# One product for the dilated values of both weight chunks, and the latent keys and values computed behind it

## What is computed

```python
dq, dk, dv, sq, sk, sv, iq, ik, iw, cq, ckv, kr = split_cols(x @ w_in)      # w_in: 1024 x 2920
...
rel = jax.nn.relu(jnp.einsum('bqhe,bse->bqhs', iqb, ik))                     # indexer, 8 heads
score = jnp.einsum('bqh,bqhs->bqs', iwb, rel)
_, idx = lax.top_k(score, n_sel)                                             # n_sel = 128
...
kv = (rms_norm(ckv, kv_norm) @ w_ukv).reshape(B, S, N_HEADS_MLA, MLA_NOPE + MLA_V)
k_nope, v = kv[..., :MLA_NOPE], kv[..., MLA_NOPE:]
```

## Time and profile before

| | us |
|---|---|
| median of 3 runs (lowest, highest) | 2184.23 (2182.27, 2187.38) |
| the profiled execution's own time | 2186.5 |
| its span in the trace | 2184.7 |
| TensorE busy | 2080.8 (95%) |
| VectorE busy | 1642.6 (75%) |
| ScalarE busy | 1409.2 (65%) |
| GpSimd busy | 581.3 (27%) |

### The profile page before, as it was taken

How to read it: one execution, slowest core, us unless ns; L and a number is a source line. 1 busy time by engine, 2 the same in 40 slices (tenths; PEclk the granted TensorE clock), 3 DMA queues, 4 the chain that set the end, 5 groups by cost and what they waited for, 6 DMA issues and landing times. The chain is left out here.

```text
span 2184.7 us, 32260 instructions
## 1 busy us (share of the span) xinstructions
PE 2080.8 (95%) x10998; PEld 1689.3 (77%) x10998; DVE 1642.6 (75%) x2419; ACT 1409.2 (65%) x1778; POOL 581.3 (27%) x336
## 2 busy tenths in 40 slices
PE   6999989899999999999888999898999999999996
PEld 4778878688888888887376888777888888888862
DVE  2486453699999999998345944537999999999955
ACT  3443762488888888887045347426888888888841
POOL 0010200133443444442011021002344434434310
PEclk9999999999999999999999999999999999999998
DMA  6312213599999999995741140265999999999938
GB/s 202 97 30 72 113 67 147 196 378 377 389 378 379 375 387 386 382 382 223 302 145 59 51 162 1 76 252 192 382 378 393 378 375 382 376 382 380 379 128 359
DMA packets 136052, 572.78 MB, mean 262 GB/s; under 512 B 32356, under 2 KB 58468, under 8 KB 82712
## 3 DMA queue, kind: packets, MB, share of 16 engines
q1 hardware_dynamic: 99096, 504.37, 60.5%
q0 software_dynamic: 36864, 67.19, 8.0%
HBM read 560.41 MB, written 78.14 MB: 292 GB/s over the span
## 5 line engine op out<-in xcount | busy, mean ns | idle before, releaser
L1430 POOL DMA_INDIRECT rows<-x_rows,index x122 | 281.4, 2307 | 129.8 <-issue 69.5
L1587 DVE TENSOR_TENSOR w_next_lo<-w_next,w_hi 128x2048 fp32r<-128x2048 f32 x128 | 292.8, 2288 | 0.1
L1587 DVE TENSOR_TENSOR w_lo<-w,w_hi 128x2048 fp32r<-128x2048 f32 x124 | 285.2, 2300 | 2.0 <-ACT w_hi L1635 1.4
L1635 ACT CAST w_hi<-w 128x2048 fp32r<-128x2048 f32 x124 | 236.4, 1906 | 51.0 <-PE ps_sum L1493 51.0
L1635 ACT CAST w_hi<-w_next 128x2048 fp32r<-128x2048 f32 x128 | 243.5, 1902 | 35.4 <-PE ps_sum L1493 35.4
L1491 PE MATMUL ps_sum<-w_hi,rowsT_first_hi 128*128 128x512 f32 x512 | 208.8, 408 | 9.1 <-PEq L151 9.1
L1491 PE MATMUL ps_sum<-w_hi,rowsT_hi 128*128 128x512 f32 x512 | 208.0, 406 | 4.4 <-DVE rowsT_lo L1599 4.4
L1516 PE MATMUL ps_sum<-w_hi,hiddenT_hi 128*128 128x512 f32 x512 | 201.8, 394 | 3.9 <-DVE hiddenT_lo L1606 3.9
L1493 PE MATMUL ps_sum<-w_hi,rowsT_first_lo 128*128 128x512 f32 x512 | 202.9, 396 | 0.0
L1493 PE MATMUL ps_sum<-w_hi,rowsT_lo 128*128 128x512 f32 x512 | 202.3, 395 | 0.0
L1518 PE MATMUL ps_sum<-w_hi,hiddenT_lo 128*128 128x512 f32 x512 | 201.8, 394 | 0.0
(11 more groups left out here) (286 smaller groups left out, 5283.3 us busy)
## 6 DMA issues: line engine op xcount, KB each, us to landing
w_next<-exp_w SPq DMA_DIRECT2D x192, 1024.0 KB, 10.1
w<-exp_w SPq DMA_DIRECT2D x128, 1024.0 KB, 9.6
w_first<-exp_w SPq DMA_DIRECT2D x32, 1024.0 KB
w_last<-exp_w SPq DMA_DIRECT2D x32, 1024.0 KB
wbuf<-w_in SPq DMA_DIRECT2D x16, 1024.0 KB, 5.5
got<-y_rows SPq DMA_DIRECT2D x8, 2048.0 KB, 21.3
got<-y_rows SPq DMA_DIRECT2D x16, 1024.0 KB, 24.3
w_out_sb<-w_out SPq DMA_DIRECT2D x2, 4096.0 KB, 19.3
```

The lines of the kernel that those rows point to most:

```text
L1430: pool.indirect_dma_start(rows[0:CAP, x.slot, :], None, d["x1_rows"], bass.IndirectOffsetOnAxis(ap=index[0:CAP, x.step, 0:1], axis=0), bou ...
L1587: dve.tensor_tensor(w13_lo[x.slot][:, :, k, :], w13[x.slot][:, :, k, :], w13_hi[:, :, k, :].bitcast(F32), ALU.subtract).then_inc(S["up_lo_ ...
L1635: act.copy(w13_hi[:, :, k, :], w13[x.slot][:, :, k, :]).then_inc(S["up_hi_b" if half else "up_hi_a"], 1)
```

## The change

Three things are edited. The `dv` units of both chunks become one: per block of 128 tokens, each product takes the 2 x 192 columns of chunks 8 and 9 together, out of both slots of `w_hi` or `w_lo`. The `kn` and `mv` units leave their places between the `idx` pairs and stand between `dv` and `sqk`. And `LOWER_AT` puts `lower(10)` and `lower(11)` at later rounds. Since both slots are now read until the last `dv` unit, `split_after` names that unit for chunk 10 and for chunk 11.

```diff
     latent = [("mq", t, c) for t in range(NT) for c in range(2)]
-    latent += [("kn", h) for h in range(H_MLA)] + [("mv", t) for t in range(NT)]
...
-    u += [("dv", c, t) for c in range(2) for t in range(NT)]
+    u += [("dv", t) for t in range(NT)]
+    u += [("kn", h) for h in range(H_MLA)] + [("mv", t) for t in range(NT)]
...
-LOWER_AT = {(3, 8): 7, (2, 0): 8, (2, 7): 9, (2, 15): 10, (1, 8): 11}
+LOWER_AT = {(3, 8): 7, (2, 0): 8, (2, 7): 9, (1, 11): 10, (1, 13): 11}
...
-    split_after = {last_use[c - 2]: c for c in range(2, len(CHUNKS))}
-    split_after[place[("rest", 0, 1)]] = 1
+    last_use[8] = last_use[9]
+    split_after = {u: [c for c in range(2, len(CHUNKS)) if last_use[c - 2] == u] for u in last_use.values()}
+    split_after[place[("rest", 0, 1)]] = [1]
...
+                    elif kind == "dv":
+                        n, rows = CHUNKS[c][1], slice(x[1] * P, (x[1] + 1) * P)
+                        both = out[:, 0:2 * n].rearrange("p (b c) -> p b c", b=2)
+                        for k in range(KD):
+                            v_hi, v_lo = w_hi[:, :, k, 0:n], w_lo[:, :, k, 0:n]
+                            pe.matmul(both, xT_hi[:, k, rows], v_hi, start=(k == 0), stop=False)
+                            pe.matmul(both, xT_hi[:, k, rows], v_lo, start=False, stop=False)
+                            mm = pe.matmul(both, xT_lo[:, k, rows], v_hi, start=False, stop=(k == KD - 1))
...
-                        o = act.copy(sb["dv"][:, x[2], x[1] * 192:x[1] * 192 + 192], src[:, 0:192])
+                        o = act.copy(sb["dv"][:, x[1], :], src[:, 0:2 * CHUNKS[8][1]])
...
-                    if u in split_after:
-                        upper(split_after[u])
+                    for c in split_after.get(u, []):
+                        upper(c)
```

More of the change, by code:

```diff
@@ L311, in _projections @@
     chunk_of = {"rest": lambda x: x[1], "ik": lambda x: IK_CHUNK, "iq": lambda x: 3 + x[1] // 2,
-                "dqk": lambda x: 5 + x[1] // 2, "dv": lambda x: 8 + x[1], "sqk": lambda x: 10 + x[1] // 2,
+                "dqk": lambda x: 5 + x[1] // 2, "dv": lambda x: 9, "sqk": lambda x: 10 + x[1] // 2,
                 "sv": lambda x: 12}
     last_use = {chunk_of[x[0]](x): u for u, x in enumerate(units) if x[0] in chunk_of}
-    split_after = {last_use[c - 2]: c for c in range(2, len(CHUNKS))}
-    split_after[place[("rest", 0, 1)]] = 1
+    last_use[8] = last_use[9]
+    split_after = {u: [c for c in range(2, len(CHUNKS)) if last_use[c - 2] == u] for u in last_use.values()}
+    split_after[place[("rest", 0, 1)]] = [1]
     with ExitStack() as ctx:
@@ L393, in _ @@
                             mm = pe.transpose(out[:, t * P:(t + 1) * P], x_sb[:, t, x[1]::KD], ident)
-                    elif kind in ("rest", "dv", "sv"):
+                    elif kind == "dv":
[6 more added lines that the diff above has]
+                            mm = pe.matmul(both, xT_lo[:, k, rows], v_hi, start=False, stop=(k == KD - 1))
+                    elif kind in ("rest", "sv"):
                         t = x[-1]
```

## The result

| | before | changed |
|---|---|---|
| median (lowest, highest), us | 2184.44 (2182.27, 2187.38) | 2220.63 (2219.93, 2220.67) |
| ratio, 95% interval | | 1.0164 [1.0146, 1.0182] |
| profiled execution, span | 2184.7 | 2218.6 |

What follows compares the result with a forecast made beforehand. TensorE was taken to bound the projections. Cheaper `dv` products, moved `kn` and `mv`, two new waits and low clock put `sqk` at 196.65 against 180.39, 16.3 us a layer: 2184.2 + 32.5 = 2217, range 2206 to 2226.

Steps and rivals of the forecast that it cites:

- TensorE sets the end, and its losses arrive: In the projections TensorE, busy 90.8 of 93 us, sets the end; everything it loses or gains arrives there.
- Products of `dv`: Joined `dv` products of 384 columns, 0.17 us apart, take 16.3 us: 5.2 us less work a layer.
- `kn` and `mv`: Taking them out of the `idx` stretch moves, not saves, 8.8 us of TensorE: 1.04 a `kn`, 0.64 an `mv`.
- First wait: Ahead of `dv`, TensorE stands from 152.0 to 161.4 until `lower(9)` has split chunk 9: 9.4 us.
- earlier selection: After the score sums, VectorE's selection starts at about 122.4 instead of 125.29: 2.9 us earlier.
- TensorE's arrival: TensorE reaches `dqk` at about 116.3 instead of 121.93, 5.6 us earlier, and ends `krT` at 152.0.
- Second wait: Ahead of `mv` 2, TensorE idles some 7 us while ScalarE's `upper(11)` waits for chunk 11, `kn` copies behind it.
- Clock: Behind each wait TensorE runs at the 1.2 GHz level, 1.5 us more; lasting twice as long would give 2220 to 2223.
- The sum: `sqk` begins at 196.65 against 180.39, 16.3 us a layer, 32.5 for two: 2184.2 + 32.5 = 2217.
- Two layers: Layer 1 is taken as a repeat of layer 0, so 16.3 us is doubled to 32.5.
- Only the first wait: Rival: chunk 11 lands while TensorE still has banks, `sqk` starts at 188.0, 7.6 late: 2199; chance 0.08.
- Sums blocked entirely: Rival: GpSimd holds VectorE's 384-wide sums off entirely; selection and `sqk` come 4.9 us later than forecast: 2227; chance 0.07.

Runs made afterwards that it cites:

- the version with only the keys: Changed kernel with only `kn` between `dv` and `sqk`, `mv` back between `idx` pairs, GpSimd's rotations after the last score sum, `lower(7)` to `lower(11)` earlier: 2173.80 us, ratio 0.9950.
- the run with both waits treated: Changed kernel with `lower(8)` to `lower(11)` at earlier rounds and `upper(11)` behind the last `mv` copy: 2189.02 us, ratio 1.0016.

## Why the prediction was right, point by point

- **TensorE sets the end, and its losses arrive.** Right. Layer 0's projections ended 18.74 us later, layer 1's 37.22; the forecast had 32.5 for both. The bounds worked out in the prediction, 12.8 to 25 us a layer, would be 2210 to 2234; the range it gives, 2206 to 2226, does not follow from them. The measured 2220.6 lies in both.
- **Products of `dv`.** Right. Predicted 0.17 us apart; four units copied 4.16 us apart, 24 x 0.173.
- **`kn` and `mv`.** Over-sized. Predicted 8.8 us, measured 7.7 (183.05 to 190.73 in the run with `upper(11)` later). The sum takes only two `mv` from it, 1.3 us, and those were right at full clock (1.2).
- **First wait.** The mechanism was right. It ended later than predicted, `dv` began at 163.43 instead of 161.4, and it was shorter, 7.9 us instead of 9.4, because TensorE itself came late (next point). What made its end late is the mis-sized term of the sum, the *earlier selection*: I had 2.9 us and measured 1.0 (124.28 against 125.29). Nearly half of the miss does not come from the change: the first 384-wide sum stood 0.85 later already, at 110.46 against 109.61. The rest is in the sums: I gave five of seven the slow rate and measured 7.75 us for seven, because rotations and sums kept each other busy longer. GpSimd is the cause, as the run with later rotations shows.
- **TensorE's arrival.** Predicted at `dqk` 116.3, measured 118.16, and the first products ran at clock 0.50. I had overlooked that pauses in the `idx` stretch could bring the low clock. It cost nothing at the end, because the first wait stood behind it; `krT` ended 3.5 us later than forecast, and the wait was the shorter for it.
- **Second wait.** Right, place and cause: VectorE reached `lower(10)` at 185.54 (183.5 predicted, late by the same term), 5.8 us later the chunk was there, and `mv` 2 began at 196.05 (193.85). The 1.9 us to spare between `upper(10)` and VectorE shrank to 0.4.
- **Clock.** I charged 1.5 us for the first wait. `dv` took 19.3 us behind it (163.43 to 182.74), against 16.8 in the version with only the keys (154.02 to 170.86), where no such stretch followed: 2.5 us. `dv` was so 1.5 us longer than the 17.8 forecast and used up 1.5 of the 1.9 us to spare. Anything beyond another 0.4 us would have arrived in the sum; that this under-sized term did not is in part luck. I charged 1.5 us for the second wait too. From 196.05 to 198.20 two `mv` took 2.15 us, 0.9 more than at full clock, and from there to the last copy it took 34.45 us, before 33.52: 0.9 more. Together 1.8.
- **The sum.** 196.65 predicted for `sqk`, 198.20 measured, 1.6 late; 0.9 of the clock came behind it. 16.3 + 1.6 + 0.9 = 18.8, the 18.74 of layer 0. Without the offset of 0.85 it is 17.9, and 36.4 for both layers, close to the 36.2 of the medians.
- **Two layers.** Layer 1 took 18.48 more. The span grew by 33.9, not 37.2: what follows the last `sv` copy of layer 1 took 893.91 us before and 890.59 after (span less the time of that copy). The eleven profiles, all alike from there on, have between 890.6 and 894.7 there. I read the 3.3 us as that spread; its cause was not sought.
- **Rivals.** Only the first wait, 2199, came about in the run with `upper(11)` later (2202.76). Without its offset to the kernel before, 2.2 us, `sqk` stands at 188.5 there, where this rival has 188.0. That is 1.0 of the 3.8 us by which the run lies above 2199; the rest was not traced. Sums blocked entirely did not: seven sums beside the rotations took 2.8 us more than without them, not 6.9. The rule of the Trainium skill behind this rival (SBUF — State Buffer, terms, shared port pair) is that the loser of the port fully blocks. The traces bear it out in that both engines slow down, and not in the size: with all 6.9 us of the rotations ahead of the sums the cost would have been more than twice what was measured.

## What to carry to other kernels

A buffer freed by one join instead of two steps moves every step that refills it to one place: ask what each engine then does in a row there, and who is queued behind the one that has to wait for a DMA. Of the two waits in a row here, mending the first gives nothing (2220.55 against 2220.63), mending the second gives 18 us. And a change that loses may hold a gain: a version with the joined product came out 7 us ahead (11 with the edit to GpSimd, which alone gave nothing) once its splits had cover. And before times of two traces are compared, look for a place up to which the kernels are alike, and see how far apart the traces stand there.

## What was not expected of the hardware

A wait of 2.9 us ahead of `dv`, in the run with `lower(9)` earlier, was followed by a low clock; one of 1.6 us, in the run with both waits treated, was not. Windows from 158 to 164 us of the first and of the second:

```profile
158.00:164.00 6.00, 6.00 (x26) 6.00 (x27) 5.66 (x16) 3.60 (x4) 0.00 (x0) 0.72 0.56 175
```

```profile
158.00:164.00 6.00, 6.00 (x37) 6.00 (x36) 5.69 (x14) 3.55 (x3) 0.00 (x0) 1.00 0.59 175
```

0.72 and 1.00, with 26 and 37 products. The other waits ahead of `dv` go the same way: 2.11 us (the run with `kn` and `mv` moved, layer 0) and 2.70 (`lower(9)` earlier, layer 1) were followed by 0.50 within 2 us, and 1.07 (the kernel before) and 1.69 (`kn` and `mv` moved, layer 1) were not. In layer 1 of the run with both waits treated the wait was longer than in layer 0, and 0.50 followed:

```profile
1234.25 0.41 PE L402 MATMUL pp<-w_hi,xT_hi 128*128 128x384 f32 x1 [2.67 <-DVE w_lo L566]
```

That the length of the wait alone decides is not shown. In the changed kernel three pauses of 0.8 us, between single small products, also led to 0.50 (window 118 to 121 above). So the two layers of one execution need not be alike, and doubling layer 0 can be off by such a stretch. The rotations and the score sums slow each other: GpSimd's longer instructions took 1.2 us beside the sums and 1.0 us beside the selection, and a sum 1.11 against 0.71.
